# Moving five small SBUF tiles of a two-block transformer kernel behind the large ones

## The chip, the cores and the metric

The kernel runs on one NeuronCore of one Trainium2 chip. The metric is the device time of one launch in microseconds (us); lower is better. The kernel before took 2034.36 us in the median of three runs (2029.74 to 2043.56).

## What is computed

One sequence of 256 tokens with 1024 channels, all in float32, goes through two blocks. Cut to what matters:

```python
def reference(x, ...):
    x = first_block(x, ...)      # one layer: SSD + attention mixer, 32 experts, gate
    return second_block(x, ...)  # four layers: mixer, then swiglu

def first_block(x, ...):
    h = rms_norm(x, attn_norm_w)
    x = x + hybrid_mixer(h, ...)            # h @ w_in (1024 x 7440), SSD, attention, w_out
    h = rms_norm(x, moe_norm_w)
    x = x + hier_moe(h, ...)                # 4 groups x 8 experts, 256 wide
    gate = sigmoid(rms_norm(x, ple_norm_w) @ w_ple_gate)
    x = x + gate * (p @ w_ple)
    return rms_norm(x, final_norm_w)

def second_block(x, ...):
    for i in range(4):
        h = rmsnorm(x, norm_mix_g[i])
        x = x + mixer_i(h)                  # short conv, neighbourhood attention, Hyena, short conv
        g, u = split(rmsnorm(x, norm_ffn_g[i]) @ f_w13[i])
        x = x + (silu(g) * u) @ f_w2[i]     # 1024 -> 2 x 2816 -> 1024
    return x
```

## The kernel before

All weights come from HBM in chunks of 1 MB (128 partitions x 2048 float32), in the order in which they are used. A chunk lands in one of three slots `raw0` to `raw2`. ScalarE rounds it into the slot's high part `ring_hi` (L1864; L2152 in the expert stage), and VectorE takes the rest as the low part `ring_lo` (L2425; L3108), so that a float32 product is three fp32r products: high by high, high by low, low by high. In the expert stage there is a second set of three slots, `second_hi` and `second_lo`.

The normalized activations stand in the same manner as two tiles of 128 x 8 x 256, with channels on the partitions. One pair is `h_hi` and `h_lo`; the other, `g_hi` and `g_lo`, lies in the shared work area. The function `parts_of` (L634) takes the g pair for the operands merged, ffn0, na, hyena and ffn3, and the h pair for all others, so for the inputs of the first mixer, of the layers' projections, and of the second and third swiglu (called ffn1 and ffn2 in the code, as the first and fourth are ffn0 and ffn3).

TensorE multiplies a chunk in one of two ways. `product_f` (its matmul is L931) holds 128 x 128 of the weights stationary and streams 256 columns of h or g, 48 matmuls to a chunk. `product_t` (L950) holds the activations stationary and streams the weights. In a swiglu, one round of the loop is a gate chunk and an up chunk (96 matmuls of L931) and a down chunk (24 matmuls of L1265, 512 columns each); there are 11 rounds. In the profile, a matmul's inputs stand with the streamed one first: `proj<-h_hi,ring_hi` streams `h_hi`.

The kernel is written with an order of its own for each engine, with semaphores between them. Nothing in it is put in order by a scheduler, and no order depends on where a tile lies.

The norm works on a few small tiles. ScalarE squares x and leaves the sums in `ssq` (L1892). GpSimd makes `ms` (L1820, L1821) and from it `inv`, the inverse root, with a power of -0.5 that it reads from `neg_half` (L1822), and then a diagonal tile from `inv` and `ident` (L1825). TensorE spreads it with `ones` (L989), and VectorE copies the result to `inv_b` (L2486), a 128 x 256 tile by which projections are scaled when they leave PSUM (L2543, L2449, L3349, L3231, L3237, and L2949 and L2955 in the swiglu). `eps_col` is a bias of one element (L2006). `params` holds gains and taps by channel, and `ident` the identity for transposes (L975).

SBUF tiles are taken one after the other from a stack by `sb`, each start rounded up to 32 bytes. All other tiles are placed by hand with `at`, as offsets from `work0`, the end of the stack rounded up to 32:

```python
def sb(name, shape, dt=f32):
    return ctx.enter_context(nc.sbuf_tensor(name, shape, dt))
...
work0 = -(-nc.sbuf_base // 32) * 32
...
def at(name, shape, offset, dt=f32):
    ...
    return nc.alloc_sbuf_tensor_at(name, shape, dt, offset=work0 + offset)
...
g_hi = at("g_hi", [P, KT, SEQ], 78 * KB, f32r)
```

Of the kernel before, what the change touches and what calls it, by code (L numbers as in the profile page):

```python
# [26 lines left out]
P = 128  # L27
SEQ, D = 256, 1024
TT = SEQ // P
# [289 lines left out]
def build(nc, A, out):  # L319
# [5 lines left out]
    with ctx:  # L325
        def sb(name, shape, dt=f32):
            return ctx.enter_context(nc.sbuf_tensor(name, shape, dt))
# [8 lines left out]
        w_hi = [ring_hi[:, i, :] for i in range(RING)]  # L336
        w_lo = [ring_lo[:, i, :] for i in range(RING)]
        x = sb("x_res", [P, TT, D])
        ssq = sb("ssq", [P, TT, 2])
        ms = sb("ms", [P, TT])  # L340
        inv = sb("inv", [P, TT])
        neg_half = sb("neg_half", [P, 16])
        eps_col = sb("eps_col", [P, 1])
        h_hi = sb("h_hi", [P, KT, SEQ], f32r)
        h_lo = sb("h_lo", [P, KT, SEQ], f32r)
        ident = sb("ident_sb", [P, P])
        ones = sb("ones", [P, P])
        params = sb("params", [P, PARAM_TILES * P])
        inv_b = sb("inv_b", [P, SEQ])


        work0 = -(-nc.sbuf_base // 32) * 32
# [3239 lines left out]
```

## Time and profile before

| | us |
|---|---|
| median of 3 runs | 2034.36 |
| lowest, highest run | 2029.74, 2043.56 |
| the profiled execution, its own time | 2043.56 |
| its span, first to last instruction | 2041.8 |
| around the span | 1.76 |

The profiled execution is the slowest of the three runs. An execution's span is what the trace shows; the rest of its time lies around it. Busy time is counted for each engine by itself, so the shares of several engines add to more than one. Where TensorE is busy for a whole stretch, that stretch's length is the number of its matmuls by their spacing, and another engine's work in it costs nothing as long as it keeps up.

### The profile page before, as it was taken

To read this page: it belongs to the slowest core of one execution; us is meant where nothing else is said; L and a number is where in the kernel's file an instruction comes from. 1 tells how busy PE (TensorE), PEld (TensorE's weight loads), DVE (VectorE), ACT (ScalarE), POOL (GpSimd) and SP (SyncE) were. 2 spreads that over 40 slices of the span, in tenths; PEclk is the share of its full clock that TensorE was granted. 3 is DMA by queue.
4 is the path that set the end of the run, shared out by engine and by line. 5 is a ranking of instruction groups with operands and counts; after the bars stand their busy time and mean duration, and the time that the engine had idled before them with its cause. 6 is when DMAs were issued, how large, how long until landed. Compare 5 with 4: busy or idle time off the path is not lost.

```text
span 2041.8 us, 32534 instructions
## 1 busy us (share of the span) xinstructions
PE 1935.0 (95%) x13424; PEld 1759.5 (86%) x13424; DVE 1374.9 (67%) x1569; ACT 923.0 (45%) x990; POOL 46.3 (2%) x65
## 2 busy tenths in 40 slices
PE   6999998999999979999999999999989999999999
PEld 6998887777777769899989999987878999999998
DVE  4767975766777665766667665567997555675555
ACT  4544843655565553433445443334334333434342
POOL 0000000000000000000101000000000000000000
PEclk8998998999999999999999999999999999999999
DMA  7552341776777747555653375552324555555553
GB/s 223 182 169 86 104 157 71 296 286 254 269 289 293 259 158 201 165 165 186 199 171 125 104 238 191 185 178 91 103 83 146 178 190 187 165 165 165 188 200 106
DMA packets 243915, 366.03 MB, mean 179 GB/s; under 512 B 12566, under 2 KB 217961, under 8 KB 231401
## 3 DMA queue, kind: packets, MB, share of 16 engines
q1 hardware_dynamic: 243817, 364.64, 53.0%
q8 instruction: 72, 1.18, 0.2%
q14 instruction: 26, 0.21, 0.0%
HBM read 363.57 MB, written 1.05 MB: 179 GB/s over the span
## 4 chain that ended last, share of the span: by engine, by line
PE 67%; DVE 15%; DMA 7%; ACT 7%; issue 4%; SPq 0%; DVEq 0%; POOL 0%; ACTq 0%
PE proj L931 36%; PE acc L1265 11%; PE proj L950 8%; DMA raw<-in_w_exp_up_dram 6%; DVE ring_lo L2425 3%; PE proj L1448 2%; DVE ring_lo L3108 2%; ACT ring_hi L1864 2%; ACT ring_hi L2152 1%; ACT second_hi L2152 1%; PE acc L1418 1%; DVE second_lo L3108 1%; PE acc L1524 1%; PE acc L1278 1%; DMA raw<-in_w_in_dram 1%
## 5 line engine op out<-in xcount | busy, mean ns | idle before, releaser
L2425 DVE TENSOR_TENSOR ring_lo<-raw,ring_hi 128x2048 fp32r<-128x2048 f32 x242 | 559.9, 2317 | 228.6 <-ACT ring_hi L1864 227.6
L1864 ACT ACTIVATE ring_hi<-raw 128x2048 fp32r<-128x2048 f32 x242 | 462.1, 1913 | 465.8 <-PE proj L931 214.7
L931 PE MATMUL proj<-h_hi,ring_hi 128*128 128x256 f32 x1808 | 521.3, 288 | 15.2 <-DVE ring_lo L2425 9.6
L931 PE MATMUL proj<-h_lo,ring_hi 128*128 128x256 f32 x1808 | 508.7, 281 | 0.0
L931 PE MATMUL proj<-h_hi,ring_lo 128*128 128x256 f32 x1808 | 508.6, 281 | 0.0
L931 PEld LDWEIGHTS proj<-h_hi,ring_hi 128*128 128x128 f32 x1808 | 343.8, 190 | 28.0 <-issue 14.4
L931 PEld LDWEIGHTS proj<-h_lo,ring_hi 128*128 128x128 f32 x1808 | 344.2, 190 | 4.2 <-issue 3.2
L931 PEld LDWEIGHTS proj<-h_hi,ring_lo 128*128 128x128 f32 x1808 | 345.4, 191 | 0.0
L931 PE MATMUL proj<-g_hi,ring_hi 128*128 128x256 f32 x704 | 197.0, 280 | 4.1 <-DVE hid L2958 4.1
L931 PE MATMUL proj<-g_lo,ring_hi 128*128 128x256 f32 x704 | 196.3, 279 | 0.0
L931 PE MATMUL proj<-g_hi,ring_lo 128*128 128x256 f32 x704 | 196.2, 279 | 0.0
L931 PEld LDWEIGHTS proj<-g_hi,ring_hi 128*128 128x128 f32 x704 | 133.7, 190 | 5.3 <-issue 4.5
L931 PEld LDWEIGHTS proj<-g_lo,ring_hi 128*128 128x128 f32 x704 | 133.9, 190 | 0.8
L931 PEld LDWEIGHTS proj<-g_hi,ring_lo 128*128 128x128 f32 x704 | 133.8, 190 | 0.0
L3108 DVE TENSOR_TENSOR second_lo<-raw,second_hi 128x2048 fp32r<-128x2048 f32 x48 | 109.9, 2291 | 34.4 <-ACT second_hi L2152 34.2
L3108 DVE TENSOR_TENSOR ring_lo<-raw,ring_hi 128x2048 fp32r<-128x2048 f32 x48 | 109.2, 2289 | 22.2 <-ACT ring_hi L2152 22.0
L1918 ACT ACTIVATE silu_g<-gate_in 128x512 f32<-128x512 f32 x44 | 27.8, 632 | 199.7 <-DVE gate_in L2949 199.7
L2152 ACT ACTIVATE second_hi<-raw 128x2048 fp32r<-128x2048 f32 x48 | 92.0, 1918 | 36.6 <-DMA raw<-in_w_exp_up_dram 19.0
L950 PE MATMUL proj<-ring_hi,h_hi 128*128 128x256 f32 x320 | 93.1, 291 | 9.8 <-DVE h_lo L3016 8.6
L2152 ACT ACTIVATE ring_hi<-raw 128x2048 fp32r<-128x2048 f32 x48 | 91.1, 1914 | 21.9 <-DMA raw<-in_w_exp_gate_dram 8.4
L1265 PE MATMUL acc<-ring_hi,hid_lo 128*128 128x512 f32 x320 | 99.5, 392 | 0.0
L1265 PE MATMUL acc<-ring_hi,hid_hi 128*128 128x512 f32 x320 | 99.4, 392 | 0.0
(440 smaller groups left out, 3429.4 us busy)
## 6 DMA issues: line engine op xcount, KB each, us to landing
raw<-in_f_w_dram SPq DMA_DIRECT2D x132, 1024.0 KB, 5.0
raw<-in_w_exp_gate_dram SPq DMA_DIRECT2D x32, 1024.0 KB, 4.8
raw<-in_w_exp_up_dram SPq DMA_DIRECT2D x32, 1024.0 KB, 5.0
raw<-in_w_exp_down_dram SPq DMA_DIRECT2D x32, 1024.0 KB, 4.8
raw<-in_w_in_dram SPq DMA_DIRECT2D x29, 1024.0 KB, 5.1
raw<-in_a_w_in_dram SPq DMA_DIRECT2D x24, 1024.0 KB, 5.2
raw<-in_b_w_qkv_dram SPq DMA_DIRECT2D x12, 1024.0 KB, 5.1
raw<-in_c_w_in_dram SPq DMA_DIRECT2D x12, 1024.0 KB, 5.1
```

Source lines behind the costliest of these rows:

```text
L931: last = pe.matmul(bank[:, a, :], w[:, k, a * P:(a + 1) * P], h[:, k, :], start=(k == 0 and w is hi and h is h_h and (a == 0 or not first) ...
L950: last = pe.matmul(bank[:, t, :], h[:, k, t * P:(t + 1) * P], w[:, k, :], start=(k == 0 and w is hi and h is h_h), stop=(k == KT - 1 and h ...
L1265: last = pe.matmul(acc[:, 2 * t + m, :], h[:, k, t * P:(t + 1) * P], w[:, k, m * HALF:(m + 1) * HALF], start=(start and k == 0 and h is hi ...
L1278: last = pe.matmul(acc[:, 2 * t + m, :], h[:, k, t * P:(t + 1) * P], w[:, k, m * HALF:(m + 1) * HALF], start=False, stop=(k == 1 and h is ...
L1418: last = pe.matmul(bank, h[:, k, 0:P], w[:, k, m * HALF:(m + 1) * HALF], start=(first and k == 0 and h is hid_hi and w is hi), stop=(k == ...
L1448: last = pe.matmul(pair(v % RING), h, w, start=(k == 0 and h is h_h and w is hi), stop=(k == KT - 1 and h is h_l))
L1524: last = pe.matmul(acc[:, 2 + h, kt * SEQ + t * P:kt * SEQ + (t + 1) * P], na_probs[i % 2][:, h, t * SEQ + kt * P:t * SEQ + (kt + 1) * P], ...
L1864: act.activation(w_hi[n.slot][:, :], raw[n.slot][:, :], ACT.Copy).then_inc(hi_ready, 1)
L1918: act.activation(silu_g[:, :], gate_in[:, :, :].rearrange("p a n -> p (a n)"), ACT.Silu).then_inc(silu_ready, 1)
L2152: act.activation(dst, raw[c.slot][:, :], ACT.Copy).then_inc(hi_ready, 1)
L2425: dve.tensor_tensor(w_lo[n.slot][:, :], raw[n.slot][:, :], w_hi[n.slot][:, :].bitcast(f32), SUB)\
L3108: dve.tensor_tensor(dst, raw[c.slot][:, :], hi.bitcast(f32), SUB).then_inc(lo_ready, 1)
```

## The change

The five small tiles `ssq`, `ms`, `inv`, `neg_half` and `eps_col` are taken from the stack after the large ones instead of ahead of them. `ssq` goes between `params` and `inv_b`, the other four behind `inv_b`.

```diff
         x = sb("x_res", [P, TT, D])
-        ssq = sb("ssq", [P, TT, 2])
-        ms = sb("ms", [P, TT])
-        inv = sb("inv", [P, TT])
-        neg_half = sb("neg_half", [P, 16])
-        eps_col = sb("eps_col", [P, 1])
         h_hi = sb("h_hi", [P, KT, SEQ], f32r)
         h_lo = sb("h_lo", [P, KT, SEQ], f32r)
         ident = sb("ident_sb", [P, P])
         ones = sb("ones", [P, P])
         params = sb("params", [P, PARAM_TILES * P])
+        ssq = sb("ssq", [P, TT, 2])
         inv_b = sb("inv_b", [P, SEQ])
+        ms = sb("ms", [P, TT])
+        inv = sb("inv", [P, TT])
+        neg_half = sb("neg_half", [P, 16])
+        eps_col = sb("eps_col", [P, 1])
```

Where the tiles stand then, in bytes from the start of a partition. The last column is the remainder of the start by 512, before and after, which tells the alignment to 32, 64, 128, 256 and 512 bytes:

| tile | bytes | start before | start after | moved by | start modulo 512 |
|---|---|---|---|---|---|
| raw, ring_hi, ring_lo, x_res | | 16512 to 90240 | the same | 0 | 128, 128 |
| ssq | 16 | 98432 | 117376 | +18944 | 128, 128 |
| ms | 8 | 98464 | 118432 | +19968 | 160, 160 |
| inv | 8 | 98496 | 118464 | +19968 | 192, 192 |
| neg_half | 64 | 98528 | 118496 | +19968 | 224, 224 |
| eps_col | 4 | 98592 | 118560 | +19968 | 288, 288 |
| h_hi | 8192 | 98624 | 98432 | -192 | 320, 128 |
| h_lo | 8192 | 106816 | 106624 | -192 | 320, 128 |
| ident | 512 | 115008 | 114816 | -192 | 320, 128 |
| ones | 512 | 115520 | 115328 | -192 | 320, 128 |
| params | 1536 | 116032 | 115840 | -192 | 320, 128 |
| inv_b | 1024 | 117568 | 117408 | -160 | 320, 160 |
| work0, with g_hi at +78 KB and all others | | 118592 | 118592 | 0 | 320, 320 |

So the h pair, `ident`, `ones` and `params` change from a start that is 64 past a multiple of 128 to a multiple of 128; `inv_b` changes from a multiple of 64 to 32 past one; the five small tiles keep their alignment; and all that lies in the work area stays where it was. On each of the five engines the instructions and their waits stand in the same order in both kernels, with the same shapes and operands; the addresses alone differ.

## Rows read from the trace of the kernel before

**Rows 1.** The page: busy us, share of the span and instructions of each engine

```profile
PE 1935.0 (95%) x13424; PEld 1759.5 (86%) x13424; DVE 1374.9 (67%) x1569; ACT 923.0 (45%) x990; POOL 46.3 (2%) x65
```

**Rows 2.** Windows inside ffn0, ffn1, ffn2 and ffn3

```profile
core 0: us, PE busy (x) PEld busy (x) DVE busy (x) ACT busy (x) POOL busy (x), PEclk, DMA share, GB/s
897.00:1040.00 143.00, 143.00 (x1062) 134.97 (x1061) 92.95 (x70) 55.18 (x36) 13.63 (x8) 1.00 0.58 191
1221.00:1345.00 124.00, 124.00 (x892) 116.81 (x891) 73.62 (x60) 45.84 (x29) 0.00 (x0) 1.00 0.57 190
1580.00:1745.00 165.00, 163.66 (x1161) 153.26 (x1160) 97.48 (x79) 62.48 (x40) 0.00 (x0) 1.00 0.55 182
1883.00:2025.00 142.00, 142.00 (x1053) 133.99 (x1052) 85.11 (x69) 54.61 (x35) 0.00 (x0) 1.00 0.53 178
```

**Rows 3.** The chain that ended last, pieces in ffn0 and ffn3: start us, us

```profile
913.69 10.91 PE proj L931 x96
924.60 5.49 PE acc L1265 x24
...
1883.87 10.91 PE proj L931 x96
...
2015.07 10.91 PE proj L931 x96
```

**Rows 4.** The same chain, pieces in ffn1 and ffn2

```profile
1221.97 11.31 PE proj L931 x96
...
1339.71 11.31 PE proj L931 x96
...
1591.91 11.31 PE proj L931 x96
...
1726.47 11.31 PE proj L931 x96
```

**Rows 5.** Line L931: duration ns min/median/max, first and last start us

```profile
L931 PE MATMUL proj<-h_hi,ring_hi x1808: 275/281/1201, 19.5 to 1820.5; 128*128 128x256 f32 x181
...
L931 PE MATMUL proj<-g_hi,ring_hi x704: 275/276/468, 865.2 to 2025.5; 128*128 128x256 f32 x176
```

**Rows 6.** Tile h_hi, window 20 to 230 us (first mixer)

```profile
L931 PE MATMUL proj<-h_hi,ring_hi x396: 275/276/775, 19.5 to 229.3; 128*128 128x256 f32 x198
...
L950 PE MATMUL proj<-ring_hi,h_hi x64: 278/280/683, 126.9 to 152.7; 128*128 128x256 f32 x64
```

**Rows 7.** Tile h_hi, window 1220 to 1345 us (ffn1)

```profile
L931 PE MATMUL proj<-h_hi,ring_hi x240: 280/281/282, 1221.8 to 1344.8; 128*128 128x256 f32 x120
```

**Rows 8.** Groups by form, TensorE: count, busy us, mean ns, idle before

```profile
L950 PE MATMUL proj<-ring_hi,h_hi 128*128 128x256 f32 x320 | 93.1, 291 | 9.8 <-DVE h_lo L3016 8.6 <-DVE h_lo L2469 1.2
...
L1448 PE MATMUL proj<-second_lo,own_hi 128*128 128x512 f32 x128 | 49.8, 389 | 0.0
...
L1448 PE MATMUL proj<-ring_lo,own_hi 128*128 128x512 f32 x64 | 24.8, 388 | 0.0
```

**Rows 9.** Line L1029, a product with h_hi streamed, in the first mixer

```profile
L1029 PE MATMUL misc<-h_hi,w_dt_hi x8: 276/276/277, 99.8 to 102.2; 128*16 128x256 f32 x8
```

**Rows 10.** Groups by form, VectorE

```profile
L2469 DVE SCALAR_TENSOR_TENSOR h_lo<-acc,params,h_hi 128x256 fp32r<-128x256 f32 x72 | 30.5, 477 | 12.0 <-ACT h_hi L1881 11.8
...
L3280 DVE TENSOR_SCALAR na_probs<-na_probs,na_inv 128x256 f32<-128x256 f32 x32 | 9.1, 350 | 0.3
...
L3198 DVE SCALAR_TENSOR_TENSOR x_res<-x_res,inv,final_w 128x512 f32<-128x512 f32 x4 | 2.7, 745 | 2.8 <-POOL inv L1822 2.8
...
L3072 DVE TENSOR_SCALAR pick<-iota_slots_sb,pos 128x256 f32<-128x256 f32 x2 | 0.6, 350 | 0.0
```

**Rows 11.** Tile inv_b, VectorE: ns min/median/max

```profile
L2949 DVE TENSOR_TENSOR gate_in<-proj,inv_b x44: 690/691/692, 872.1 to 2020.6; 128x512 f32<-128x512 f32 x44
L2955 DVE TENSOR_TENSOR silu_g<-silu_g,inv_b x44: 681/683/687, 877.5 to 2026.0; 128x512 f32<-128x512 f32 x44
L2543 DVE TENSOR_TENSOR pj<-proj,inv_b x17: 679/684/692, 28.1 to 241.1; 128x512 f32<-128x512 f32 x17
L2449 DVE TENSOR_TENSOR pj<-proj,inv_b x16: 690/691/692, 772.6 to 1798.4; 128x512 f32<-128x512 f32 x16
L3349 DVE TENSOR_TENSOR h_raw<-proj,inv_b x12: 679/684/693, 1396.5 to 1531.4; 128x512 f32<-128x512 f32 x12
...
L3237 DVE TENSOR_TENSOR pj<-proj,inv_b x4: 691/692/692, 1066.1 to 1118.5; 128x512 f32<-128x512 f32 x4
```

## The prediction, made before the changed kernel ran

> **What bounds the kernel now.** I read the page first, for the engines' shares; then windows inside the long loops; then the chain of work that ended last through them; and then, since the change is one of addresses alone, the durations of instructions of one shape by the tile that they read, to see whether any of them depends on where a tile lies.
>
> The page shows TensorE busy for 95% of the span, VectorE for 67%, ScalarE for 45% and GpSimd for 2% [rows 1]. In windows inside the four swiglu loops TensorE is busy 572.66 of 574 us (143.00, 124.00, 163.66 and 142.00 of them), at a granted clock of 1.00, which is the 2.4 GHz level, while VectorE works for 61% of the time (349.16 us) [rows 2]. There the time is the number of matmuls by their spacing, and nothing else. The chain says the same: in ffn0 and ffn3 it is made of pieces of 96 matmuls of L931 and 24 of L1265 by turns, 10.91 and 5.49 us long [rows 3].
>
> The one thing that the reader should stop at is that the 96 matmuls don't take the same time in all four loops. In ffn0 and ffn3 they take 10.91 us, 113.6 ns each [rows 3]; in ffn1 and ffn2 they take 11.31 us, 117.8 ns each [rows 4]. Shape, type, count and granted clock are the same. What differs to the eye is the streamed tile: g in the faster two, h in the slower two. The single durations repeat it: the median is 276 ns with g streamed and 281 ns with h [rows 5], and in ffn1 all of them lie between 280 and 282 [rows 7]. I call these the short and the long spacing. The change moves the h pair and leaves g alone, so here it could matter, if anywhere.
>
> **The change, part by part.**
>
> The instructions. None is added, removed or moved on any engine, no wait is added and none goes, and no DMA changes its size or place in a queue. This term is 0, and nothing hides behind that: there is no edit of the work.
>
> The h pair, 192 bytes lower. It now starts at a multiple of 128, and at the same remainder by 512 as the ring tiles. Two observations bear on the spacing. First, h shows both spacings at its old place: in the first mixer the median of the L931 matmuls that stream it is 276 ns [rows 6], in ffn1 it is 281 [rows 7]. One address with two speeds means that the start of the tile doesn't choose the speed; the place in the program does. Second, g and h have the same start modulo 512 before the change (320) and still differ by loop [rows 3, 4], so what tells them apart isn't the low bits of the address, and only those change: each slice of 1024 bytes of h begins in the same block of 512 bytes as before. As for the relation of the streamed tile to the stationary one: the expert products stream the second set (start 320 modulo 512) or the ring (128) against `own_hi` (320), so the two starts agree in the first case and don't in the second, and they take 389 and 388 ns [rows 8]. L1029 streams h against `w_dt_hi`, which start alike modulo 512, and takes 276 ns, the shorter of the two durations [rows 9]. After the change h and ring start alike. Neither relation has a price of its own in these rows.
>
> The trace can't show h at its new place, so I bound it from both sides. L931 streams h in 3 x 1808 = 5424 matmuls [rows 5], 56.5 rounds of 96, and a round is worth 11.31 - 10.91 = 0.40 us [rows 3, 4]. Gain at most: in the first mixer at least half of 396 x 3 = 1188 matmuls are at the short spacing already [rows 6], 6.2 rounds, which leaves 50.3 rounds, 20.1 us; the 3 x 320 = 960 matmuls of L950 that hold h stationary [rows 8], with a median of 280 even in the mixer [rows 6], add 10 rounds, 4.0 us. Together 24.1 us. Loss at most: 17 rounds of ffn1 and ffn2 are on the long spacing as they are (8 from 1221.97 to 1339.71, 9 from 1591.91 to 1726.47) [rows 4]; the other 39.5 rounds by 0.40 us are 15.8 us. I take 0, since the nearest rows, the same tile at both speeds, say that the speed isn't a matter of its address.
>
> Here a rule of the Trainium skill is worth a look. Its page "TensorE: Matmul & The Clock Gate", section "Wait — 56ns, not 53.3ns?", gives back-to-back matmuls one spacing, their columns over the clock and about 2.5 ns, with no term for an address. For 256 columns at 2.4 GHz that is 109.2 ns, an estimate from the page. The trace doesn't agree: it has 113.6 and 117.8 ns. By the page there would be no second spacing, and the two rivals on spacing below would fall away; the sum would be 0 as it is here. The measurement decides, so they stay.
>
> `inv_b`, now 32 past a multiple of 64. VectorE reads it in 44 + 44 + 17 + 16 + 12 + 4 = 137 instructions of 512 columns at 683 to 692 ns [rows 11]. The nearest row for an input that starts 32 past a multiple of 64 is `iota_slots`, in L3072: 350 ns for 256 columns, and the same operation on `na_probs`, which starts at a multiple of 64, takes 350 as well [rows 10]. So 0. As the upper end I take the dearest VectorE instruction of 512 columns in the groups read, 745 ns [rows 10], against 691: 54 ns by the 49 instructions outside the swiglu are 2.6 us if all of them lay on the path. Inside, the 88 others would add 4.8 us to an engine that has 39% of its time free there, beside a TensorE that never stops [rows 2], and cost nothing. Below nothing it can't well be: 683 to 692 ns is what other tiles of that shape take.
>
> `params`, `ident`, `ones`. They are read as one scalar by partition, or 128 columns at a time. L2469 reads `params` and `h_hi` in 477 ns [rows 10]; as the upper end, 5 ns more for its 72 is 0.4 us. The five small tiles keep their alignment and are touched by GpSimd, 46.3 us in all [rows 1], at the same instructions. These are 0.
>
> The sum is 0 on the profiled execution's own 2043.56 us (its span 2041.8 and 1.76 around it), so it stays at 2043.56. That execution was the slowest of three; the median is 2034.36, and with no term to add the prediction is that median, 2034.4 us. The ends of the unknown terms are -24.1 and 15.8 + 2.6 + 0.4 = +18.8 us.
>
> **The rivals.**
>
> A: the long spacing falls away where h is streamed or held. For it speaks that ffn1 and ffn2, with h, are long and ffn0 and ffn3, with g, are short [rows 3, 4]; two against two, and the move is of h alone. Against it, the same h is short in the mixer [rows 6], and g agrees with h in the low bits. If only the 17 rounds of rows 4 turn, the gain is 6.8 us; the bound is 24.1. Between these ends I price it at 15: 2019 us.
>
> B, on the other side: the long spacing spreads. The two spacings look like two ways in which weight loads and matmuls fall into step, and each holds for a whole loop once it is entered. With h elsewhere, stretches that now fall into the short one (the first mixer, rows 6) could fall into the long. It decides as soon as more rounds turn long than turn short, and costs 0.40 us a round: at most 15.8 us, 2050 us, which is slower by 0.8%. To be slower by over 1% it would need a third spacing, which no row shows.
>
> C: reads of `inv_b` off a multiple of 64 are dearer. By rows 11 and the dearest row it is 2.6 us, 2037 us. To reach 1% it would take 0.4 us more in each of the 49 instructions outside the swiglu, against a row that shows 0 [rows 10].
>
> D: the tiles don't end up where the code says, or the alignment is of no use because `work0` moves too. The stack ends in the same rounded place, so `work0` stays; this one I rule out.
>
> **How the numbers follow.** No measurable effect, with a median of new runs between 2028 and 2042: 0.80. A: 0.08. B: 0.08. C: 0.02. Something that no row shows, of either sign: 0.02. Three runs spread over 0.7%, so what a measurement can tell from no change is about 1%. From A, only its far end (over 20 us, so nearly all rounds turned) is faster by over 1%: with half of it, and a share of the unseen, 0.05. B ends at 0.8%; with the unseen, with C's far end and with new runs that come out high, slower by over 1% is 0.06. Within 1% is 0.89. The range runs from 2019 (A) to 2050 (B's bound), and takes in nearly all of the no-effect case.
>
> **What would show it right or wrong.** Right: the chain in ffn0 and ffn3 again has pieces of 10.91 us, in ffn1 and ffn2 of 11.31; L2949 stays at 691 ns and L2955 at 683; L931 with h keeps its median of 281 over the whole run. A would show as pieces of 10.91 in ffn1 and ffn2, and a median of 276 for h. B would show as a median of 281 for the first mixer. C would show in the six rows of `inv_b`. The prediction is wrong if the time leaves 2014 to 2055, and its reasoning is wrong if the time stays but the spacing of g, which the change doesn't touch, is another.

## The result, and the profile after

The changed kernel takes 2055.73 us (median of 5 runs, 2051.49 to 2060.33), the kernel before 2034.36 (5 runs, 2029.74 to 2043.56). The ratio is 1.0102, with a 95% interval of 1.0069 to 1.0136. So the change costs 21 us, where I forecast none, and the time lies above the range that I gave.

The profiled execution after took 2061.14 us, its span 2059.3, which is 17.5 us more than the span of before. The page's line of engines, after:

```profile
PE 1951.1 (95%) x13424; PEld 1777.5 (86%) x13424; DVE 1376.0 (67%) x1569; ACT 922.7 (45%) x990; POOL 46.3 (2%) x65
```

Against [rows 1] the counts are the same, and of the engines only TensorE works longer: its matmuls by 16.1 us, its weight loads by 18.0. VectorE has 1.1 us more, ScalarE 0.3 less. So no work was added, and TensorE's own time makes up all but 1.4 us of the longer span: the same matmuls take longer.

Which ones, the chain says. First ffn0, with g streamed, then ffn1, ffn2 (h) and ffn3 (g); columns as in [rows 3]:

```profile
924.87 10.91 PE proj L931 x96
935.78 5.49 PE acc L1265 x24
...
1235.12 11.52 PE proj L931 x96
1246.64 5.51 PE acc L1265 x24
...
1606.46 11.52 PE proj L931 x96
...
1901.42 10.91 PE proj L931 x96
```

With g nothing has changed: 10.91 us, as in [rows 3]. With h a round of 96 takes 11.50 to 11.52 us, 120 ns a matmul, where it was 11.31 or 117.8 ns [rows 4]. That is neither the short spacing nor the long one. It is a third.

It holds wherever h is read in matmuls of 256 columns, not in those loops alone. First L931 and L950 by line, then tile h_hi in the window 20 to 230 us (the first mixer); the median duration is the middle one of three:

```profile
L931 PE MATMUL proj<-h_hi,ring_hi x1808: 277/283/1202, 19.7 to 1838.0; 128*128 128x256 f32 x181
...
L931 PE MATMUL proj<-g_hi,ring_hi x704: 275/277/467, 876.4 to 2043.0; 128*128 128x256 f32 x176
...
L950 PE MATMUL proj<-ring_hi,h_hi x320: 278/283/682, 130.1 to 1867.6; 128*128 128x256 f32 x160
```

```profile
L931 PE MATMUL proj<-h_hi,ring_hi x396: 278/283/683, 19.7 to 229.5; 128*128 128x256 f32 x198
```

With h streamed the median is now 283 ns over the run and in the mixer, where [rows 5] had 281 and [rows 6] 276. With h held (L950) it is 283 as well, against 280 in [rows 6]; g has 277 against 276. The three durations go with the three spacings: 276 with 113.6 ns, 281 with 117.8, 283 with 120.

The size follows from the groups by form of both kernels; the first three lines are the kernel before:

```profile
L931 PE MATMUL proj<-h_hi,ring_hi 128*128 128x256 f32 x1808 | 521.3, 288 | 15.2 <-DVE ring_lo L2425 9.6 <-DVE hid L2958 4.1 <-DVE h_lo L2469 1.3
L931 PE MATMUL proj<-h_lo,ring_hi 128*128 128x256 f32 x1808 | 508.7, 281 | 0.0
L931 PE MATMUL proj<-h_hi,ring_lo 128*128 128x256 f32 x1808 | 508.6, 281 | 0.0
```

```profile
L931 PE MATMUL proj<-h_hi,ring_hi 128*128 128x256 f32 x1808 | 525.1, 290 | 13.7 <-DVE ring_lo L2425 9.1 <-DVE hid L2958 3.4 <-DVE h_lo L2469 1.2
L931 PE MATMUL proj<-h_lo,ring_hi 128*128 128x256 f32 x1808 | 513.0, 284 | 0.0
L931 PE MATMUL proj<-h_hi,ring_lo 128*128 128x256 f32 x1808 | 512.8, 284 | 0.0
L950 PE MATMUL proj<-ring_hi,h_hi 128*128 128x256 f32 x320 | 94.1, 294 | 8.7 <-DVE h_lo L3016 8.0 <-DVE h_lo L2469 0.8
```

The three groups with h streamed grew from 1538.6 to 1550.9 us, by 12.3; L950's first from 93.1 [rows 8] to 94.1, by 1.0, and its two others by 1.2 and 1.3. Together that is 15.8 us. These are sums of durations that overlap one another. Counted without overlap, the matmuls that read h in L931 and L950 make up 14.3 of TensorE's 16.1 us, and L1418 in the expert stage, which doesn't read h, another 3.1 (other lines lose some).

The delay can also be followed through the run. The same instruction starts later after the change by 11.2 us at the start of ffn0 (first g matmul, 865.2 [rows 5] against 876.4), by 11.2 inside it (913.69 [rows 3] against 924.87), by 17.2 when L2449 runs last (1798.4 [rows 11] against 1815.6), by 17.55 inside ffn3 (1883.87 [rows 3] against 1901.42) and by 17.5 at its end (L2949 runs last at 2020.6 [rows 11] and 2038.1). The loops with g add nothing.

Not all of that delay is the change's. The expert stage, from the first L1448 to the end of the last L1418, took 362.1 us in this profile of before and 371.2 in this one of after, so 9.1 of the first 11.2 us come from it. It has no matmul of L931 or L950. L1448, which holds h in a part of it, streams 512 columns, and where its matmuls with h follow without a gap they start 229.4 to 229.6 ns apart before and 229.2 after. Two further profiles of before have 367.6 and 364.8 us for the stage, a second one of after 362.7. A part of its chain, 35% from 400 to 700 us, is the arrival of weights (`in_w_exp_up`), and the stage's length varies from one execution to the next. With the stage left out, the three profiles of before take 1679.7, 1662.5 and 1666.7 us and the two of after 1688.1 and 1693.4. The means lie 21 us apart, as the medians do. So a single pair of profiles shows where the matmuls got slower; how much it costs is read from the medians.

In this pair of profiles the first mixer seems free: L931 with h starts last in its window at 229.3 us [rows 6] and at 229.5. The granted clock tells why. Windows after, columns as in [rows 2]:

```profile
20.00:241.00 221.00, 218.12 (x1697) 200.58 (x1697) 164.12 (x250) 107.88 (x124) 0.00 (x0) 0.99 0.45 145
...
500.00:780.00 280.00, 255.33 (x1213) 210.68 (x1214) 182.25 (x149) 155.31 (x166) 5.58 (x10) 0.97 0.66 239
```

Before, the same windows had 0.97 and 0.99. The two differences are of like size and opposite, and the mean over the span is 0.981 before and 0.982 after, so the clock doesn't make the total.

`inv_b`, the second tile that lost its alignment, in VectorE's first line on it after:

```profile
L2949 DVE TENSOR_TENSOR gate_in<-proj,inv_b x44: 691/692/694, 883.3 to 2038.1; 128x512 f32<-128x512 f32 x44
```

The median is 692 ns against 691 [rows 11], and L2955's 684 against 683: that term is nothing.

### The profile page after: what moved, and what is told of

Same layout as the page of the kernel before. It is cut to its first block, busy times and chain, and to the rows that moved or that the text cites. A ratio compares the mean times of both kernels' runs of the same rounds, so it can differ in the third digit from the quotient of the medians.

```text
span 2059.3 us, 32534 instructions
## 1 busy us (share of the span) xinstructions
PE 1951.1 (95%) x13424; PEld 1777.5 (86%) x13424; DVE 1376.0 (67%) x1569; ACT 922.7 (45%) x990; POOL 46.3 (2%) x65
## 4 chain that ended last, share of the span: by engine, by line
PE 58%; DVE 13%; DMA 6%; ACT 5%; issue 3%; DVEq 0%; POOL 0%; ACTq 0%
PE proj L931 31%; PE acc L1265 11%; PE proj L950 6%; DMA raw<-in_w_exp_up_dram 6%; DVE ring_lo L2425 3%; PE proj L1448 2%; DVE ring_lo L3108 2%; ACT ring_hi L2152 1%; ACT second_hi L2152 1%; PE acc L1418 1%; DVE second_lo L3108 1%; ACT ring_hi L1864 1%; PE acc L1524 1%; PE acc L1278 1%; PE proj L1716 1%
## 5 line engine op out<-in xcount | busy, mean ns | idle before, releaser
L2425 DVE TENSOR_TENSOR ring_lo<-raw,ring_hi 128x2048 fp32r<-128x2048 f32 x242 | 560.2, 2318 | 230.0 <-ACT ring_hi L1864 229.4
L931 PE MATMUL proj<-h_hi,ring_hi 128*128 128x256 f32 x1808 | 525.1, 290 | 13.7 <-DVE ring_lo L2425 9.1
L931 PE MATMUL proj<-h_lo,ring_hi 128*128 128x256 f32 x1808 | 513.0, 284 | 0.0
L931 PE MATMUL proj<-h_hi,ring_lo 128*128 128x256 f32 x1808 | 512.8, 284 | 0.0
L931 PEld LDWEIGHTS proj<-h_hi,ring_hi 128*128 128x128 f32 x1808 | 347.0, 192 | 26.3 <-issue 13.6
L931 PEld LDWEIGHTS proj<-h_lo,ring_hi 128*128 128x128 f32 x1808 | 347.0, 192 | 4.2 <-issue 3.1
L931 PEld LDWEIGHTS proj<-h_hi,ring_lo 128*128 128x128 f32 x1808 | 347.0, 192 | 0.0
L931 PE MATMUL proj<-g_hi,ring_hi 128*128 128x256 f32 x704 | 197.2, 280 | 4.1 <-DVE hid L2958 4.1
L931 PE MATMUL proj<-g_hi,ring_lo 128*128 128x256 f32 x704 | 196.4, 279 | 0.0
L931 PE MATMUL proj<-g_lo,ring_hi 128*128 128x256 f32 x704 | 196.3, 279 | 0.0
L931 PEld LDWEIGHTS proj<-g_hi,ring_hi 128*128 128x128 f32 x704 | 134.0, 190 | 5.3 <-issue 4.4
L931 PEld LDWEIGHTS proj<-g_lo,ring_hi 128*128 128x128 f32 x704 | 133.9, 190 | 0.8
L931 PEld LDWEIGHTS proj<-g_hi,ring_lo 128*128 128x128 f32 x704 | 133.7, 190 | 0.0
L950 PE MATMUL proj<-ring_hi,h_hi 128*128 128x256 f32 x320 | 94.1, 294 | 8.7 <-DVE h_lo L3016 8.0
L1265 PE MATMUL acc<-ring_hi,hid_lo 128*128 128x512 f32 x320 | 99.6, 393 | 0.0
L1265 PE MATMUL acc<-ring_lo,hid_hi 128*128 128x512 f32 x320 | 99.4, 392 | 0.0
```

The costliest lines, as they stand in the source:

```text
L931: last = pe.matmul(bank[:, a, :], w[:, k, a * P:(a + 1) * P], h[:, k, :], start=(k == 0 and w is hi and h is h_h and (a == 0 or not first) ...
L950: last = pe.matmul(bank[:, t, :], h[:, k, t * P:(t + 1) * P], w[:, k, :], start=(k == 0 and w is hi and h is h_h), stop=(k == KT - 1 and h ...
L1265: last = pe.matmul(acc[:, 2 * t + m, :], h[:, k, t * P:(t + 1) * P], w[:, k, m * HALF:(m + 1) * HALF], start=(start and k == 0 and h is hi ...
L2425: dve.tensor_tensor(w_lo[n.slot][:, :], raw[n.slot][:, :], w_hi[n.slot][:, :].bitcast(f32), SUB)\
```

## Experiments

In all that follows, D is the start of the streamed tile less the start of the held one, in bytes, modulo 256 (a matmul streams one and holds the other; every slice of either starts a multiple of 512 further on, so D is the same for all slices). Before the change D is 192 for h and for g over the ring (320 - 128); after it, 0 for h. In L950 the roles are swapped, the ring is streamed and h held: D is 64 before and 0 after. In the kernels with an edit in `build`'s allocations, `put(name, shape, offset)` is `sb` with the place written out; tiles not shown stay at their place or only make room, and the lines of four kernels (h_only, inv_only, ring_up, h_first) are numbered 3 higher: their L934 is L931, their L1268 is L1265.

### Which tile

Each half of the change alone.

```diff
-        h_hi = sb("h_hi", [P, KT, SEQ], f32r)
+        h_hi = put("h_hi", [P, KT, SEQ], 98432, f32r)
-        h_lo = sb("h_lo", [P, KT, SEQ], f32r)
+        h_lo = put("h_lo", [P, KT, SEQ], 106624, f32r)
```

> Only h_hi and h_lo stand where the change put them (start 128 modulo 512, as the ring); ident, ones, params and inv_b stand as before. Theory S (the whole loss is a third matmul spacing of 120 ns wherever h is streamed or held): the swiglu pieces of ffn1 and ffn2 are 11.5 us as after the change, g pieces 10.91, and the time is that of the changed kernel, 1.010 of before (0.6 to 1.4%). Rival I (inv_b off a multiple of 64, or params, costs the time): within 0.3% of before, and h's spacing is back at 113 and 118 ns.

Measured: 2051.7 us (2048.67 to 2061.62), ratio 1.0104 (1.0073 to 1.0134). Its chain in ffn1:

```profile
1240.45 11.50 PE proj L934 x96
...
1257.44 11.52 PE proj L934 x96
```

The h pair alone is the whole loss. And the other half, with `inv_b` 32 past a multiple of 64 and h at its old remainder:

```diff
-        inv_b = sb("inv_b", [P, SEQ])
+        inv_b = put("inv_b", [P, SEQ], 98464)
```

> Only inv_b starts 32 past a multiple of 64 here; the h pair keeps its old start modulo 1024 (320), 1024 bytes higher. Theory S: time within 0.3% of before, L2949 691 ns, L2955 683 ns, pieces 10.91 and 11.31 us. Rival I: 0.5 to 1% slower than before with the old matmul spacing.

Measured: 2031.99 us (2023.51 to 2037.83), ratio 0.9984 (0.9971 to 0.9997), and

```profile
L2952 DVE TENSOR_TENSOR gate_in<-proj,inv_b x44: 691/692/692, 868.2 to 2014.6; 128x512 f32<-128x512 f32 x44
```

So `inv_b` costs nothing. In this run ffn0 and ffn1 had 10.91 us and ffn2 and ffn3 11.31: the two old spacings aren't tied to g and h.

### Its address, or its distance from the ring

h's place of before is kept (modulo 512) and the ring moves up by 192, so that D is 0 for h and for g too, which nothing had touched (`x_res`, behind the ring, goes up by 192 with it).

```diff
-        ring_hi = sb("ring_hi", [P, RING, CHUNK], f32r)
-        ring_lo = sb("ring_lo", [P, RING, CHUNK], f32r)
+        ring_hi = put("ring_hi", [P, RING, CHUNK], 41280, f32r)
+        ring_lo = put("ring_lo", [P, RING, CHUNK], 65856, f32r)
```

> h stays at its old start (320 modulo 512); ring_hi, ring_lo and x go up by 192 so that they too start at 320. Theory R (what counts is how the streamed tile's start stands to the stationary tile's: equal modulo 64 to 512 gives 120 ns): h spacing 120 ns, pieces of 11.5 us in ffn1 and ffn2 and, as g also starts at 320, in ffn0 and ffn3 too: some 35 us slower than before. Theory A (what counts is h's own start, a multiple of 128): h at 113 and 118 ns as before, time within 0.5% of before, or faster if the ring as a streamed tile gains from it.

Measured: 2061.17 us (2058.56 to 2068.73), ratio 1.0145 (1.0117 to 1.0173). Its chain in ffn0, where g is streamed:

```profile
933.20 11.51 PE proj L934 x96
```

All four loops have 11.51. g, at its old address, has the third spacing as soon as the ring's start agrees with its own. The cross-check puts h ahead of the ring: h at 41088, the ring at 57664 (D is 64 for h, 0 for g).

```diff
-        ring_hi = sb("ring_hi", [P, RING, CHUNK], f32r)
+        ring_hi = put("ring_hi", [P, RING, CHUNK], 57664, f32r)
-        h_hi = sb("h_hi", [P, KT, SEQ], f32r)
+        h_hi = put("h_hi", [P, KT, SEQ], 41088, f32r)
```

> The h pair starts at 128 modulo 512 as after the change, but the ring starts at 320: the two differ by 192 again, with the roles swapped. Theory R: h at 113 and 118 ns, time as before. Theory A: h at 120 ns, pieces of 11.5 us in ffn1 and ffn2, 1% slower than before. The ring against g (320) is equal here: by R g goes to 120 ns, pieces of 11.5 us in ffn0 and ffn3; by A g stays at 10.91 us.

Measured: 2052.16 us (2048.88 to 2055.11), ratio 1.009 (1.0068 to 1.0111). ffn0 (g), then ffn1 (h):

```profile
931.19 11.51 PE proj L934 x96
...
1244.21 11.31 PE proj L934 x96
```

The loss has gone over from the loops with h to those with g, as the distance did. It is the relation of the two starts that counts, and neither start by itself: h at its new place is off 11.51 as soon as the ring stands elsewhere, and the ring at 64 modulo 256 gives 11.51 with g and 11.31 with h.

### Other distances in the kernel

Four kernels with other values of D. For h_128 and h_64 only the h pair moves, to 98560 and 98496; in g96_h32 the ring moves up by 96 and h down by 64; in both_128 the ring moves up by 64.

```diff
-        h_hi = sb("h_hi", [P, KT, SEQ], f32r)
+        h_hi = put("h_hi", [P, KT, SEQ], 98560, f32r)
```

> The start of the streamed tile less that of the stationary one, modulo 512, is called D. So far D = 0 gave 120 ns, D = 192 gave 113 or 118, D = 320 gave 118 (h streamed) or 114 (ring streamed). Here h starts 128 above the ring: D = 128 with h streamed, 384 with h stationary; all else as before. Theory R with a period of 128 bytes (or 64): h at 120 ns, time 1% above before, as after the change. Theory R with a period of 256 or 512: h is off 120 ns, between 113 and 118, time within 0.6% of before or faster. Theory A (h at a multiple of 128 is slow): 120 ns.

> h starts 64 above the ring: D = 64 streamed, 448 stationary; all else as before. Theory R with a period of 256: D = 64 is the same as 320, so h streamed is at 118 ns (mean 117.6) and ring streamed with h stationary, 448, is the same as 192: pieces of 11.31 us in ffn1 and ffn2, time 0 to 0.5% above before. Period 128: D = 64 is the same as 192, so the time is that of before, with h at 113 and 118. Period 64: 120 ns and 1% slower.

> The ring goes up by 96 and h stands 32 above it: D = 32 with h streamed, 96 with g streamed. If the two streams disturb each other only when they start in one and the same block, 32 is still off 120 ns and 96 too. If it is a matter of distance (the closer, the worse), h at 32 is nearer to 120 than g at 96. Time: 0.5 to 1.5% slower than before if g leaves 113 ns (each ns on its 2112 matmuls is 2.1 us, on the 5424 of h 5.4 us).

> The ring goes up by 64 and h stays at its old start less nothing (320), so that h, g and all other products of the work area stand 128 modulo 512 above the ring. Theory R with a period of 128: all at 120 ns, as with the ring at 320, 1.4% slower than before. With a period of 256 or 512: all off 120 ns; if 128, the farthest from equal in a period of 256, is the best, faster than before by 0.3 to 1.5%.

Measured:

| kernel | D of h, g | us | ratio (95%) | 96 of L931 with h | with g |
|---|---|---|---|---|---|
| h_128 | 128, 192 | 2051.36 | 1.0112 (1.0068 to 1.0156) | 11.52, 11.39 | 10.91 |
| h_64 | 64, 192 | 2043.33 | 1.0058 (1.0025 to 1.009) | 11.31 | 10.91, 11.31 |
| g96_h32 | 32, 96 | 2054.61 | 1.0122 (1.0076 to 1.0168) | 11.21 | 11.51 |
| both_128 | 128, 128 | 2062.8 | 1.0156 (1.011 to 1.0203) | 11.52, 11.39 | 11.52 |

The chain of g96_h32 in ffn0, then ffn1; and of both_128 in ffn0:

```profile
930.22 11.51 PE proj L931 x96
...
1246.30 11.21 PE proj L931 x96
1257.51 5.62 PE acc L1265 x24
```

```profile
938.63 11.52 PE proj L931 x96
950.15 5.58 PE acc L1265 x24
```

No other distance among these is better than before's 192. h_64 has the long one of the old spacings in both loops with h, and is 0.6% slower for it. h_128 and both_128 missed what I had expected of a period of 256 bytes: D = 128 was to lie off 120 ns, and 120 ns had been my sign of a period of 128. The next bench decides between the two. The last pieces show that L1265 (512 columns) moves as well: 5.62 and 5.58 us, against 5.49 in [rows 3], since the ring that it streams stands elsewhere to `hid`.

### The distance by itself

A bench without the layer: TensorE repeats rounds of 96 matmuls of L931's shape and pattern, one line of the program for each D in steps of 16 bytes (D = 16 i on line 99 + i), then 48 of 512 columns (D = 32 i on line 132 + i), and the output is zeros.

```diff
+            def narrow(d):
+                return [t[:, d // 4:d // 4 + KT * COLS].rearrange("p (k n) -> p k n", k=KT) for t in (all_hi, all_lo)]
+            for i in range(16):
+                product(32 * i, mm[32 * i])
+            for i in range(16):
+                d = 32 * (7 * i % 16)
+                product(d, mm[d])
```

> The cost by itself. This kernel leaves out the whole computation and stores zeros: it loads one slice of w_in as the streamed tile and one as the stationary tile, splits both into high and low parts, and then only runs matmuls, in the order of product_f (96 of 256 columns per stretch, start of the streamed tile D bytes above the stationary one modulo 512; a line of its own for each D). First D = 0, 32, ... 480, then the same in scrambled order, then D = 16, 48, ... 496, then the order of the down chunk (512 columns) for D = 0, 32, ... 480. Theory R, period 256: 96 matmuls (192 to a line and pass) at 0 and 256 take 120 ns each, at 64 and 320 118, at 128 and 384 119, at 192 and 448 113 to 116, alike in both passes. Rival, that the speed hangs on the rest of the kernel (other engines' reads, waits, DMAs): no pattern with D, one spacing for all. For 512 columns: R says a pattern too, with D = 320, the place in the kernel, at 229 ns, and perhaps a D at 220.

Measured, at a granted clock of 1.00 (the first piece holds the rise of the clock). The chain; in the first pass D goes 0 (L99), 32 (L101), 96 (L105), 192 (L111), 256 (L115):

```profile
17.08 13.17 PE proj L99 x96
30.25 11.31 PE proj L101 x96
...
52.87 11.51 PE proj L105 x96
...
87.04 10.91 PE proj L111 x96
...
109.30 11.52 PE proj L115 x96
...
199.87 11.51 PE proj L99 x96
...
268.36 10.89 PE proj L119 x96
...
313.33 11.31 PE proj L111 x96
...
415.12 10.94 PE proj L106 x96
...
562.30 10.92 PE acc L132 x48
573.22 11.20 PE acc L133 x48
584.42 11.00 PE acc L134 x48
```

The kernel's three spacings are all here, with no layer around them: 11.51 at D = 0 (L99, L115), 10.91 and 11.31 both at 192 (L111, twice). The full list, us for 96 matmuls, of the first pass, the scrambled one and the odd steps:

| D | 0 | 16 | 32 | 48 | 64 | 80 | 96 | 112 |
|---|---|---|---|---|---|---|---|---|
| us | 11.51 | 11.20, 11.39 | 11.21, 11.31 | 11.36 | 10.89, 11.31 | 11.52 | 11.51 | 10.94 |

| D | 128 | 144 | 160 | 176 | 192 | 208 | 224 | 240 |
|---|---|---|---|---|---|---|---|---|
| us | 11.39 | 11.39 | 11.26, 11.39 | 11.44 | 10.91, 11.31 | 11.44 | 11.35 | 11.25 |

From D = 256 on the values come again within 0.02 us, but for 272, which had 11.39 where 16 had 11.20. A period of 128 is out: 96 has 11.51 and 224 has 11.35, 112 has 10.94 and 240 has 11.25. Several distances have more than one value; at 64 and 192 the two are some 0.40 us apart. The 512-column matmuls have another pattern, in which D = 0 is the best of all: 10.92 / 48 = 227.5 ns, against 229 at 64 (L134) and 233 at 32 (L133).

### Two spacings at one distance

The kernel before, profiled again with no edit:

> The kernel before, profiled once more. If each loop's spacing is set by addresses and order alone, the pieces are the same to 0.02 us: 10.91 in ffn0 and ffn3, 11.31 in ffn1 and ffn2. If a start with D = 192 can fall into either of two rhythms from run to run, some of the four change sides, and the runs' spread (2021 to 2044 us) is partly this.

> The kernel before, a third profile: each of ffn1 and ffn2 is at 10.91 or 11.31 us in all its rounds (the first profile had both long, the second both short), ffn0 and ffn3 too; span 2027 to 2042 us.

Measured: 2031.86 and 2033.28 us. The chain of the second profile in ffn1, and of the third in ffn0 and ffn1:

```profile
1237.39 10.91 PE proj L931 x96
1248.30 5.49 PE acc L1265 x24
```

```profile
926.80 11.31 PE proj L931 x96
...
1237.59 10.91 PE proj L931 x96
```

In the second profile all four loops are short, in the third only ffn0 is long; in the first it was ffn1 and ffn2 [rows 4]. So the loop that is long changes from one execution to the next of one program. Each shows 8 or 9 pieces of 96, so that it is worth some 3.5 us. The changed kernel was profiled again as well:

> The changed kernel, profiled again: D = 0 has one rhythm only, so h's L931 is again at 119.8 ns on the mean and the pieces of ffn1 and ffn2 at 11.46 to 11.51 us.

Measured: 2057.93 us, the loops with h at 11.50 and 11.52 again, the median of L931 with h at 283 again; ffn0 (g) at 10.91 and ffn3 (g) at 11.31. The third spacing comes every time, while the two others take turns.

What picks between the two? In the kernel each round of L931 follows 24 matmuls of L1265. A second bench has rounds of 96 at each D, each followed by 24 of 512 columns, with D = 64, 0 and 192 for these in its three parts.

```diff
+                for d in steps:
+                    for turn in range(2):
+                        product(d, mm[d])
+                        down(after, mb[after])
```

> The swiglu's round by itself: the whole computation is left out (zeros are stored) and TensorE runs 96 matmuls of 256 columns with D, 24 of 512 columns with D = 64 (as 320, the kernel's), and both again; D from 0 to 240 in steps of 16; then all again with 512-column D = 0 and 192. From the first bench: 11.51 us at D = 0 and 96, 11.39 at 128, 10.9 or 11.31 at 64 and 192, depending on what ran before. If the rhythm is handed over from the 512-column matmuls, D = 192 after 64 is 10.91 or 11.31 in both of its pieces, and another 512-column D changes which; if it is drawn anew at each start, the two pieces of one D differ. A D that gives 10.9 after all three is the robust place. Pieces of 24: 5.49 us at 64, 5.44 at 0, 5.60 at 192.

Measured. The chain, the pieces at D = 192 (L111), behind 512-column pieces at 64, at 0 and at 192:

```profile
422.90 11.31 PE proj L111 x96
...
961.29 11.31 PE proj L111 x96
...
1501.85 10.89 PE proj L111 x96
```

In this execution the choice follows from the pieces between, alike in both rounds of each part. D = 64 is short behind 64 (10.88) and long behind 0 and 192 (11.31). D = 0, 80 and 96 have 11.51 or 11.52 and D = 112 has 10.92 or 10.93 behind all three, while D = 16 has 11.20, 11.39 and 10.88: there the distance of the 96 alone doesn't fix the time. The same in the kernel, with `hid`, the held tile of L1265, moved by 128 or by 320 (with four tables of the Hyena stage that share its room):

```diff
-        hid_hi = at("hid_hi", [P, 2, SEQ], 44 * KB, f32r)
+        hid_hi = at("hid_hi", [P, 2, SEQ], 44 * KB + 128, f32r)
```

> hid_hi and hid_lo stand 128 bytes higher (and, to make room, four Hyena tables too), so that the down chunks, which stream the ring against them, have D = 192 in place of 320. If 512 columns follow the pattern of 256, they go from 229 ns to 220 (256 columns went from 118 to 114): 44 pieces of 24 matmuls in the swiglu stages go from 5.49 to 5.28 us, 0.21 x 44 = 9 us, and the kernel is 0.3 to 0.6% faster than before. If the 512 column matmuls don't care, it is within 0.2%.

> hid_hi and hid_lo stand 320 bytes higher (with four Hyena tables), so that the down chunks have D = 0: by the bench 227 ns in place of 229 for 512 columns, pieces of 5.44 us in place of 5.49, 44 x 0.05 = 2.2 us and as much again in the expert stage if that waited for TensorE. h and g stay at D = 192; if the 512-column matmuls hand them the short rhythm, all four loops are at 10.91 and the kernel is 0.3 to 0.6% faster than the median of before; if they hand them the long one, all four are at 11.31 and it is 0.3 to 0.5% slower.

Measured: 2039.73 us, ratio 1.0053 (1.0027 to 1.0078), for 128; 2045.85 us, ratio 1.007 (1.0045 to 1.0096), for 320. The chains in ffn0, hid_up and then hid_zero:

```profile
941.07 11.31 PE proj L931 x96
952.38 5.60 PE acc L1265 x24
957.98 10.90 PE proj L931 x96
```

```profile
935.67 11.31 PE proj L931 x96
946.98 5.44 PE acc L1265 x24
```

With `hid` at distance 0, L1265 is at its best (5.44) and every round of L931 but the last of ffn1 is long, as in the bench; the saving of 0.05 us a piece is paid for with 0.40 a round. At distance 192 the rounds alternate, where the bench had them short. What I had expected of hid_up failed too: pieces of 24 of L1265 at 5.28 us and a faster kernel; they take 5.60, and it is slower. Before's own 64 gives 5.49, and either spacing.

### A distance with one short spacing

D = 112 gave 10.92 to 10.94 in both benches and nothing else, so it could end the changes from run to run. A tile can't be put there by `sb`; three kernels do it with one wide tile that is sliced 16 bytes in: the ring (ring_208), the ring and `hid` (ring_208_hid), and the h pair (h_112).

```diff
-        h_hi = sb("h_hi", [P, KT, SEQ], f32r)
-        h_lo = sb("h_lo", [P, KT, SEQ], f32r)
+        hh = put("h_both", [P, 4 + 2 * KT * SEQ], 98528, f32r)
+        h_hi, h_lo = [hh[:, 4 + u * KT * SEQ:4 + (u + 1) * KT * SEQ].rearrange("p (k n) -> p k n", k=KT) for u in range(2)]
```

> Out of the bench: D = 112 is the one place at which 96 matmuls took 10.92 to 10.94 us after each of the three 512-column patterns. Here the ring starts at 208 modulo 256 (80 bytes up, one tile for high and low), h stays at 64, g, ssd and attn are at 64 as ever: D = 112 for everything that is streamed against the ring. All four swiglu loops at 10.92 us a round, the mixer's and the projections' L931 at 113.7 ns. Products that stream the ring have D = 144 in place of 320: 512 columns 5.60 us in place of 5.49 (44 pieces, 4.8 us lost), 256 columns 118.7 in place of 117.7. Against before with about half of its h matmuls long (2700 x 4.4 ns = 12 us): 4 to 10 us faster, ratio 0.995 to 1.000. If D = 112 is robust only in the bench, slower by 0.2 to 0.8%.

> The same, with hid_hi and hid_lo 144 bytes up as well, so that the down chunks have D = 0 (5.44 us a piece). Pieces 10.92 and 5.44: a swiglu round of 16.36 us against 16.40 or 16.80 before. 7 us better than ring_208 over 44 rounds: ratio to before 0.991 to 0.997.

> In the bench the stationary tile stood at a multiple of 32 and the streamed one was shifted; in ring_208 it was the other way round, and D = 112 took 11.52 us. Here only the h pair is shifted (start 240 modulo 256, one tile), the ring stays at 128 as in the bench. If the bench holds for a streamed tile off a multiple of 32: ffn1 and ffn2 at 10.92 us in each round, h's L931 at 113.7 ns on the mean, kernel 0 to 0.6% faster than before (before's h mean is 114.8 to 116.6). If a start off 32 is the trouble itself: 11.5 us, 1% slower, as in ring_208.

Measured: ring_208 2067.34 us, ratio 1.017 (1.0139 to 1.0201); ring_208_hid 2063.39 us, 1.0156 (1.0126 to 1.0185), with pieces of L1265 at 5.55 and not 5.44; h_112 2037.18 us, 1.0022 (1.0003 to 1.004). The chain of ring_208 in ffn0, then of h_112 in ffn1 with h_112's line of L950:

```profile
935.59 11.52 PE proj L931 x96
```

```profile
1240.47 10.94 PE proj L931 x96
```

```profile
L950 PE MATMUL proj<-ring_lo,h_both x320: 277/283/415, 125.5 to 1843.9; 128*128 128x256 f32 x160
```

With the ring off a multiple of 32 (208 modulo 256) the expectation failed: 11.52, the worst of the list. That ring is the held tile; in h_112, as in the bench, the held tile stands at a multiple of 32 and the streamed one 16 past it, and 10.94 comes as expected. The time gains nothing all the same: before has 10.91 in most of its loops, and the 960 matmuls of L950, which hold h, now off 32, have a median of 283 ns against 279 to 280 before. Their starts lie 120.0 ns apart on the mean where they follow without a gap, against 117.2 to 117.7 in the three profiles of before, which is 2 to 3 us. The rest of the 5 us between the medians isn't explained. No kernel in the study is faster than before by as much as 1%.

## Why the prediction was wrong

**The step that failed** is the h pair, priced at 0: "I take 0, since the nearest rows, the same tile at both speeds, say that the speed isn't a matter of its address". The pair's price is the whole result (h_only, 1.0104). The step had three supports.

1. "One address with two speeds means that the start of the tile doesn't choose the speed." The observation was right: at D = 192 there are two spacings (before_again, before_third, the bench). The conclusion was not. Two values at one distance say nothing of what another has, and D = 0 has one, above both.
2. "g and h have the same start modulo 512 before the change and still differ by loop". True, and for the same reason beside the point: their distance from the ring was the same too. I compared cases that agreed in what the change was about to alter.
3. "Neither relation has a price of its own in these rows." This one asked the right question, of the wrong rows. L1448 [rows 8] has 512 columns, and there D = 0 is the cheapest in the bench; L1029 [rows 9] holds 16 columns, not 128. For 256 columns over a held tile of 128 columns I used no row at D = 0.

**The bounds.** The loss was bounded at 39.5 rounds by 0.40 us, 15.8 us, with the two spacings that the rows had as its only values; I wrote that over 1% "would need a third spacing, which no row shows". It came. All 56.5 rounds go to 11.51: for rounds from the long spacing that is 0.20 us, from the short one 0.60. From the profile of before, with 17 long rounds in ffn1 and ffn2 and the rest short, it is at most 17 x 0.20 + 39.5 x 0.60 = 27 us, and the ten rounds of L950 could add up to 6. Not all of the rest were short there: the three groups with h grew by 12.3 us, and L950's three by 3.5. The measured 17.5 us of span and 21.4 us between the medians lie below that. The starts of h's matmuls that follow without a gap (under 160 ns) lie 116.6, 114.8 and 115.3 ns apart on the mean in the three profiles of before, and 119.9 in both of after. By 5424 that is 18 to 28 us, an estimate that leaves out L950; the third spacing is enough to carry the result. The loss bound had also left out L950, which the gain bound counted, and the range ended at 2050, though the ends of my own terms summed to +18.8, 2053 us. An honest upper end would have been worked out without a ceiling on the spacing, since the trace had no row for this pair of starts.

**B** had the place right, all of L931 with h, the first mixer too, where the median went from 276 to 283, and the direction. It was mis-sized: a round that was short costs 0.60 us and not 0.40, and one that was long pays 0.20 as well. Of its picture, that each spacing "holds for a whole loop once it is entered", the runs show that it holds in most, and alternates in hid_up.

**A** didn't come: the long spacing fell away nowhere through the change.

**C**, `inv_b`: right at 0. inv_only has 0.9984 (0.9971 to 0.9997) and 692 ns. `params`, `ident` and `ones` at their new remainder have no run of their own. h_only leaves them at their old places and has the whole loss (1.0104 against 1.0102), so nothing measurable is left for them or for the five small tiles: right at 0, as were the instructions, whose counts are the same.

**What would show it.** I had set 281 as the sign of B and an unchanged spacing of g as the sign that the reasoning held. g's spacing stayed, in most loops, and the reasoning was wrong: it looked at the tile that the change didn't touch. The figure that told was a round of 11.51, which stood in no list of mine.

A rule of the Trainium skill can be held against these runs. Its page "SBUF — State Buffer", section "Who interferes with whom", gives TensorE two independent read ports, one for the moving operand and one for the weight load, and says that "PE and ACT never wait on anyone". The section speaks of engines that wait for one another; read for the two reads of one engine, it leaves no term for where two tiles stand, and the change would cost 0. The runs don't agree: with TensorE busy without a gap, 96 equal matmuls took 10.89 to 11.52 us by the distance of the two starts. That the two reads hinder each other would be a reading of this; no run here shows what inside the chip takes the time.

## What to carry to other kernels

Where TensorE is the bound and each matmul has its own weight load, as these fp32r matmuls have, the start of the streamed tile relative to the held one, modulo 256, is part of the kernel's speed: a change that only moves allocations can cost 1% or more, and ought to be read as one that touches every such matmul. So list the two starts of each hot pair before and after, and if the new pair's difference occurs nowhere in the trace in the same shape, say that its price is unknown, and measure it in a bench of one line for each difference. A case that shows two speeds with the suspected cause unchanged doesn't clear that cause.

## What the runs showed that I had not expected

- The spacing of 256-column matmuls, each with a load of 128 columns, depends on the distance of the starts, with a period of 256 bytes: from 113.4 to 120 ns, 5.8%, in the bench and in the kernel at D = 0, 32, 64, 96, 112, 128 and 192. At 0, 80, 96 (long) and 112 (short) all rounds without a gap agree within 0.03 us, where the held tile starts at a multiple of 32; at 16, 32, 64, 128, 144, 160, 192 and 208 there is more than one, from 0.1 to 0.5 us apart.
- At the kernel's own distance, 192, and in the bench at 64, the same instructions have two stable spacings, 113.6 and 117.8 ns. At 192 one program takes either from one execution to the next, for a whole loop; that is 3.5 us a loop, and can be a part of the 0.7% over which the runs of before spread. The 512-column pieces between pass one or the other on: at their distance 0 always the long one, in bench and kernel. What picks behind pieces at 64, as in the kernel before, and why hid_up alternates, stays open.
- 512-column matmuls have another order: D = 0 is the best (227.5 ns), 32 among the worst (233).
- A held tile that starts off a multiple of 32 bytes behaves as though it stood elsewhere: at a distance of 112 it had 11.52 us, the one at a multiple of 32 had 10.94. 11.52 is near what D = 96 has (11.51), as if the start were rounded up to the next 32. The one other place is L950 in h_112, which holds h at 240 modulo 256: 120.0 ns, the 11.52 us that D = 128 can have, where D = 144 had 11.39 or 11.20. That agrees, but no run was made to test it.
- fp32 reads of VectorE that start 32 past a multiple of 64 cost 1 ns or nothing in 692.
